# Expert layer of a decoder trunk: transpositions and gather in halves, second matrix loaded with four consecutive rows per partition

## The reference, cut to what matters

```python
def swiglu(h, w1, w3, w2):
    return (jax.nn.silu(h @ w1) * (h @ w3)) @ w2
...
def moe_swiglu(h, router, w1, w3, w2):
    logits = (h @ router).astype(F32)
    top_v, top_i = lax.top_k(logits, TOP_K)
    gates = jax.nn.softmax(top_v, axis=-1)
    ...
    for e in range(N_EXPERTS):
        y = y + swiglu(h, w1[e], w3[e], w2[e]).astype(F32) * dense_gate[..., e:e + 1]
```

## Time and profile before

| | us |
|---|---|
| median of three runs | 1545.33 |
| the profiled execution | 1544.98 |
| its span, first to last instruction | 1543.2 |
| experts, from the first piece's products to the end (608.8 to 1543.2) | 934.4 |
| second full job (724.87 to 850.48) | 125.6 |
| one small job (1073.70 to 1185.40) | 111.7 |

### The profile page before, as it was taken

One profiled execution on the slowest core, in us unless ns is written; L12 is line 12 of the kernel. 1 busy time (PEld: TensorE's weight loads), 2 busy tenths in 40 slices (PEclk: granted clock), 3 DMA queues, 4 the chain that ended last, 5 costly groups with the idle time before them and its releaser, 6 DMA issues.

```text
span 1543.2 us, 19252 instructions
## 1 busy us (share of the span) xinstructions
PE 1453.4 (94%) x7350; PEld 1154.3 (75%) x7350; DVE 1115.5 (72%) x1172; ACT 926.3 (60%) x938; POOL 51.9 (3%) x64
## 2 busy tenths in 40 slices
PE   7999999999999999999999999899899899898996
PEld 5776779999886577888888767667668677677675
DVE  1515255555362337988898899998998998998997
ACT  2222344344232134776776787897887887878885
POOL 0330000000032000000000000000000000000000
PEclk9999999999999998999999999999999999999998
DMA  9522615550833081998999999999999999999990
GB/s 323 184 87 86 223 46 180 188 186 22 269 138 110 0 339 58 350 368 325 354 368 361 348 406 402 388 388 400 392 397 383 401 396 388 404 395 385 396 374 27
DMA packets 141701, 433.46 MB, mean 281 GB/s; under 512 B 5694, under 2 KB 30420, under 8 KB 141652
## 3 DMA queue, kind: packets, MB, share of 16 engines
q1 hardware_dynamic: 141460, 432.25, 74.4%
q0 software_dynamic: 192, 0.53, 0.1%
HBM read 431.71 MB, written 1.05 MB: 280 GB/s over the span
## 4 chain that ended last, share of the span: by engine, by line
PE 60%; DVE 20%; issue 13%; ACT 5%; DMA 0%; SPq 0%; DVEq 0%; ACTq 0%
PE bank L1798 19%; DVE ring_lo L1309 14%; PE bank L1387 12%; PE bank L1364 7%; PE bank L1369 6%; PE bank L1823 4%; PE bank L1649 4%; ACT w_hi L821 3%; PE bank L1353 1%; DVE h L1154 1%; PE bank L1343 1%; PE bank L1691 1%; DVE at_hi L1281 1%; PE bank L1544 1%; ACT memT L777 1%
## 5 line engine op out<-in xcount | busy, mean ns | idle before, releaser
L1309 DVE TENSOR_TENSOR ring_lo<-ring,w_hi 128x2048 fp32r<-128x2048 f32 (+1 forms) x352 | 754.7, 2187 | 77.4 <-ACT w_hi L821 76.7
L821 ACT ACTIVATE w_hi<-ring 128x2048 fp32r<-128x2048 f32 (+1 forms) x352 | 636.4, 1842 | 171.6 <-PE bank L1798 170.7
L1798 PE MATMUL bank<-w_hi,xg 128*128 128x512 f32 x1120 | 408.2, 395 | 3.1 <-DVE ring_lo L1309 3.1
L1798 PE MATMUL bank<-ring_lo,xg 128*128 128x512 f32 x896 | 363.6, 406 | 31.4 <-DVE ring_lo L1309 27.1
L1798 PEld LDWEIGHTS bank<-w_hi,xg 128*128 128x128 f32 x1120 | 211.3, 189 | 47.3 <-DVE ring_lo L1309 3.5
L1798 PEld LDWEIGHTS bank<-ring_lo,xg 128*128 128x128 f32 x896 | 168.5, 188 | 104.4 <-DVE ring_lo L1309 71.0
L1798 PE MATMUL bank<-ring_lo,at_hi 128*128 128x512 f32 x448 | 182.1, 406 | 25.7 <-DVE at_hi L1281 24.4
L1798 PE MATMUL bank<-w_hi,at_hi 128*128 128x512 f32 x448 | 176.2, 393 | 0.0
L1798 PEld LDWEIGHTS bank<-ring_lo,at_hi 128*128 128x128 f32 x448 | 84.0, 187 | 63.9 <-DVE ring_lo L1309 47.4
L1095 DVE TENSOR_TENSOR wf_lo<-ring,wf_hi 128x1024 fp32r<-128x1024 f32 x66 | 80.5, 1223 | 60.0 <-ACT wf_hi L718 60.0
L718 ACT ACTIVATE wf_hi<-ring 128x1024 fp32r<-128x1024 f32 x66 | 69.6, 1058 | 70.4 <-PE bank L1387 68.8
(11 more groups left out here) (326 smaller groups left out, 1591.6 us busy)
## 6 DMA issues: line engine op xcount, KB each, us to landing
ring<-in_moe_w SPq DMA_DIRECT2D x168, 2048.0 KB, 9.7
ring<-in_ffn_w SPq DMA_DIRECT2D x18, 1536.0 KB, 6.8
ring<-in_w_in SPq DMA_DIRECT2D x6, 2048.0 KB, 15.1
ring<-in_w_out SPq DMA_DIRECT2D x8, 1024.0 KB, 5.0
ring<-in_ffn_w SPq DMA_DIRECT2D x3, 2048.0 KB, 7.7
ring<-in_w_in SPq DMA_DIRECT2D x4, 1024.0 KB, 15.4
ring<-in_xa_wkv SPq DMA_DIRECT2D x2, 2048.0 KB, 15.4
ring<-in_w_in SPq DMA_DIRECT2D x2, 1184.0 KB, 7.4
```

Source lines behind the costliest of these rows:

```text
L821: act.activation(w_hi[:, i % NB, 0:cols.stop - cols.start], ring[:, slot_of(u), cols], ACT.Copy)\
L1309: dve.tensor_tensor(ring_lo[slot_of(u)][:, cols], ring[:, slot_of(u), cols], w_hi[:, i % NB, 0:cols.stop - cols.start], sub).then_inc(S["l ...
L1798: ins = mm(dst[:, :], st_, mv, start=opens, stop=closes, skip_group_check=small)
```

## The change

Six edits.

1. `turn`, `small_silu`, `turned_hi`, `small_hidden` and `turned_lo` take a half x, and their semaphores count halves (`hn`) instead of chunks. In small jobs ACT's and DVE's steps for the second half stand one piece after those of the first; `rows1` of chunks 2 and 3 moves by one piece.
2. On TensorE, in small jobs, `turn(d-1, 1)` is done after the first piece of the w3 rows instead of directly behind `turn(d-1, 0)`; for chunk 3, half 0 comes after p37 as before and half 1 after p38. TensorE waits for `j_t` of each half ahead of that half's products.
3. The gather is cut: kt 0 to 3 before p40, kt 4 to 7 between p41 and p42; `j_gps` is raised after the second half.
4. The copy `hotT` moves from DVE (ahead of `gather_lo`) to ACT (ahead of `gather_hi`).
5. w2 units: partition p gets rows 4p to 4p+3, one run of 16 KB; transposition f takes columns f, f+4, f+8 ... of its half (a stationary operand read with a step of 16 bytes).
6. `keep_busy`: (6, 6) becomes (6, 3) ahead of `sel_ready`, and (4, 6) becomes (4, 4) ahead of the jobs.

```diff
-def rows1_at(d):
+def rows1_at(d, small):
-    return last_piece(1, d) + NB + 1
+    return last_piece(1, d) + NB + 1 + (small and d > 0 and CHUNKS[d - 1] == 2)
...
-def turned_at(d):
+def turned_at(d, x, small):
+    if small:
+        return JOB_PIECES - 2 + x if d == NCH - 1 else last_piece(1, d + 1) + NB + 1 + x
     return JOB_PIECES - 2 if d == NCH - 1 else last_piece(1, d + 1) + NB + 1
...
-                    sp.dma_start(dst, src.rearrange("e (k p) c -> p (e k) c", p=P)).then_inc(arrived[slot_of(u)], 16)
+                    rows_by = "e (p k) c -> p (e k) c" if w == 2 else "e (k p) c -> p (e k) c"
+                    sp.dma_start(dst, src.rearrange(rows_by, p=P)).then_inc(arrived[slot_of(u)], 16)
... (ACT; DVE has the same turns(i) with turned_lo and small_hidden)
+                def turns(i):
+                    for d in range(NCH):
+                        for x in halves(d):
+                            if i == turned_at(d, x, small) + (small or d == NCH - 1):
+                                turned_hi(d, x)
+                        for x in halves(d):
+                            if small and i == turned_at(d, x, small):
+                                small_silu(d, x)
...
+                turns(JOB_PIECES)
+                act.wait_ge(S["j_gtps"], j1)
+                act.activation(hotT[:, :, :], v3(ps[0], 0, 256, 2), ACT.Copy).then_inc(S["j_gt"], 1)
                 gather_hi(j2)
... (DVE)
-                dve.wait_ge(S["j_gtps"], j1)
-                dve.tensor_copy(hotT[:, :, :], v3(ps[0], 0, 256, 2)).then_inc(S["j_gt"], 1)
+                turns(JOB_PIECES)
                 gather_lo(j2)
... (TensorE)
-            keep_busy(6, 6)
+            keep_busy(6, 3)
...
-            def gather(n):
+            def gather(n, b):
                 pe.wait_ge(S["j_g"], n)
-                for kt in range(KT):
+                for kt in range(4 * b, 4 * b + 4):
...
-                i.then_inc(S["j_gps"], 1)
+                if b:
+                    i.then_inc(S["j_gps"], 1)
...
-            keep_busy(4, 6)
+            keep_busy(4, 4)
...
+                        if then is not None and cols.start == 0:
+                            then()
...
-                            rows = slice(FC * x + P * f, FC * x + P * f + P)
+                        rows = slice(FC * x + f, FC * x + FC, 4)
...
-                    turn(d - 1)
-                    rows_of(3, d)
-                    pe.wait_ge(S["j_t"], cn[d - 1])
+                    turn(d - 1, 0)
+                    later = None
+                    if CHUNKS[d - 1] == 2:
+                        if small:
+                            later = lambda: turn(d - 1, 1)
+                        else:
+                            turn(d - 1, 1)
+                    rows_of(3, d, later)
...
-                        products(2, d - 1, part)
-                        if d == NCH - 1 and part == 0:
-                            turn(d)
+                        later = None
+                        if d == NCH - 1 and part:
+                            turn(d, 0)
+                            if small:
+                                later = lambda: turn(d, 1)
+                            else:
+                                turn(d, 1)
+                        pe.wait_ge(S["j_t"], hn[d - 1][part])
+                        products(2, d - 1, part, later)
...
-                gather(j2)
-                pe.wait_ge(S["j_t"], cn[NCH - 1])
-                products(2, NCH - 1, 0)
-                products(2, NCH - 1, 1).then_inc(S["j_yps"], 1)
+                for part in range(2):
+                    gather(j2, part)
+                    pe.wait_ge(S["j_t"], hn[NCH - 1][part])
+                    ins = products(2, NCH - 1, part)
+                ins.then_inc(S["j_yps"], 1)
```

More of the change, by code:

```diff
@@ L38 @@
 CHUNK0 = tuple(FC * sum(CHUNKS[:d]) for d in range(NCH))
+HALF0 = tuple(sum(CHUNKS[:d]) for d in range(NCH))
+HALVES = sum(CHUNKS)
 MAX_JOBS = N_EXP + 3
@@ L768, in job @@
                 cn = [act.snap(j * NCH + (c + 1)) for c in range(NCH)]
+                hn = [[act.snap(j * HALVES + (HALF0[d] + x + 1)) for x in range(CHUNKS[d])] for d in range(NCH)]
                 j1, j2, pieces = act.snap(j + 1), act.snap(j + 2), act.snap(j * JOB_PIECES + len(FFN_PIECES))
@@ L784, in small_rows3, with small_silu, turned_hi @@
                     i.then_inc(S["j_a"], 1)
[L786 to L800, removed]
-                    i.then_inc(S["j_th"], 1)
+                def small_silu(d, x):
+                    act.wait_ge(S["j_tps"], hn[d][x])
+                    act.activation(s_sil[x], ps[4 + x][:, 0:256], ACT.Silu).then_inc(S["j_hid"], 1)
+                def turned_hi(d, x):
+                    act.wait_ge(S["j_m" if small else "j_tps"], hn[d][x])
+                    if d == NCH - 1 and x:
+                        act.wait_ge(S["j_gtps"], j1)
+                    if small:
+                        i = act.activation(at_hi[:, 4 * x:4 * x + 4, 0:SMALL], s_act[x], ACT.Copy)
+                    else:
+                        i = act.activation(at_hi[:, 4 * x:4 * x + 4, :], v3(ps[4 + x], 0, 512, 4), ACT.Copy)
+                    i.then_inc(S["j_th"], 1)
+                def turns(i):
[6 more added lines that the diff above has]
+                                small_silu(d, x)
                 for i in range(JOB_PIECES):
@@ L806, in job @@
                             yrow_out(j, half)
+                    turns(i)
                     for d in range(NCH):
[L808 to L813, removed]
+                        if i == rows1_at(d, small):
                             rows1(d)
@@ L1257, in job @@
                 cn = [dve.snap(j * NCH + (c + 1)) for c in range(NCH)]
+                hn = [[dve.snap(j * HALVES + (HALF0[d] + x + 1)) for x in range(CHUNKS[d])] for d in range(NCH)]
                 j1, j2, pieces = dve.snap(j + 1), dve.snap(j + 2), dve.snap(j * JOB_PIECES + len(FFN_PIECES))
@@ L1266, in rows3, with small_hidden, turned_lo, turns @@
                     i.then_inc(S["j_a"], 1)
[L1267 to L1271, removed]
                     for x in halves(d):
[L1273 to L1283, removed]
-                    i.then_inc(S["j_t"], 1)
+                        dve.sem_inc(S["j_m"], 1)
+                        dve.sem_inc(S["j_hid"], 1)
+                def small_hidden(d, x):
+                    dve.wait_ge(S["j_hid"], hn[d][x])
+                    dve.tensor_tensor(s_act[x], v3(s_sil[x], 0, 256, 4), v3(ps[4 + x], 256, 512, 4), mult)\
+                       .then_inc(S["j_m"], 1)
+                def turned_lo(d, x):
+                    dve.wait_ge(S["j_th"], hn[d][x])
+                    fs = slice(4 * x, 4 * x + 4)
+                    if small:
+                        i = dve.tensor_tensor(at_hi[:, fs, SMALL:P], s_act[x], at_hi[:, fs, 0:SMALL], sub)
+                    else:
+                        i = dve.tensor_tensor(at_lo[:, fs, :], v3(ps[4 + x], 0, 512, 4), at_hi[:, fs, :], sub)
+                    i.then_inc(S["j_t"], 1)
+                def turns(i):
+                    for d in range(NCH):
+                        for x in halves(d):
+                            if i == turned_at(d, x, small) + (small or d == NCH - 1):
+                                turned_lo(d, x)
+                        for x in halves(d):
+                            if small and i == turned_at(d, x, small):
+                                small_hidden(d, x)
                 for i in range(JOB_PIECES):
@@ L1771, in job, with products @@
                 cn = [pe.snap(j * NCH + (c + 1)) for c in range(NCH)]
+                hn = [[pe.snap(j * HALVES + (HALF0[d] + x + 1)) for x in range(CHUNKS[d])] for d in range(NCH)]
                 j1, j2, pieces = pe.snap(j + 1), pe.snap(j + 2), pe.snap(j * JOB_PIECES + len(FFN_PIECES))
-                def products(w, d, part):
+                def products(w, d, part, then=None):
                     u = UNIT_OF[w, d, part]
```

30 lines of the change are left out of this document (17 added, 13 removed).

## The result

Four runs of the changed kernel took 1624.97 us in the median (1615.97 to 1626.6), four of the kernel before beside them 1545.53 (1545.2 to 1546.16). The ratio is 1.0501, interval 1.0484 to 1.0519: 5% slower, where the prediction had 0.3% faster. The profiled execution has a span of 1624.8 us against 1543.2, and its mean granted TensorE clock is 0.965.

What follows compares the result with a forecast made beforehand. Full jobs were taken as bound by TensorE, small jobs by a saturated DVE with six pauses. Small jobs -3.3, full jobs +1.2 and ahead of the jobs -1.9 sum to -4.0: from 1545.33 to 1541.3 us, range 1532 to 1550.

Steps and rivals of the forecast that it cites:

- Columns f, f+4, ...: Weight loads of the turns, read with a 16-byte step: no change taken; bounds no change and half pace, doubling the turn.
- The third rival: Stepped loads in the turns at half pace: 10.5 us a small job, 63 in all; about 1610 us; 8 in 100.
- Turns in halves: Small jobs: -0.4 us each at turn(1) and turn(2); at turn(3) a 1.42 pause goes and 0.32 comes at p42.
- Gather in halves: Small jobs: pauses 2.33 at p43, 1.86 at `gather_lo`, 0.25 at p2; +0.64 with turn(3), net +0.3 with `hotT`.
- `hotT` off DVE: Small jobs: moving this copy from DVE to ACT was to save DVE 0.33 us by starts.
- Full jobs: TensorE waits 0.6 us at p40 after the gather's first half; two jobs +1.2 us, between 0 and +2.6.
- Ahead of the jobs: Three fewer idle matmuls before the selection: -1.9 us; with the clock back later, between -2.0 and +1.6.
- Runs of 16 KB: DMA of w2 units: 0 taken; faster landings worth 0, slower ones covered up to 4 us a job.
- Rival 2: Gather's second half costs more if turns give under 0.3 us a job: 1548.7 or 1550.6 us; 15 in 100.
- Rival 1: DVE's pauses at the turns vanish: 3.3 us more a small job, about 20 in all, 1521 us; 16 in 100.

## Why the prediction was wrong

**The step that failed** is "Columns f, f+4, ...": "I take no change, since the float32 load already takes some two cycles of 2.4 GHz for each column and a second line a column may fit into that." It doesn't. The upper bound given there, a load at half the pace which doubles the turn, is what came: half a turn 3.53 us for 1.75, a pair of load and matmul 0.22 us for 0.11, a load in itself 330 ns for 192. The term that was put at 0 was 85 us in the changed kernel. The argument for the lower bound rested on no row, since the trace had no load with a step; it was a guess on how two costs overlap. The prediction quotes the cacheline rule of the Trainium skill (Advanced Engine Details and Errata, "SBUF Cachelines"), by which each access on a different line pays. It spoke against the edit. The price as a mechanism of this kernel was reckoned at 65 us against a forecast gain of 4, and it was given 8 in 100. With both bounds open and nothing in the trace between them, it should have had several times that.

**The third rival** was the mechanism, and its sizes can be checked. It spoke of three turns and a half but added 3.5 x 3 = 10.5 us a small job. The doubled turns measured 12.5 us on TensorE, of which 10.75 reached the job. That 10.5 came so near is luck: one half too few was counted, and nothing was taken off for what DVE's stock still covers. It forecast 6 us for the transposes of the full jobs at 0.11 each. There the loads do get slower, as the load group of those transposes shows in the kernel after (shortest, median, longest in ns; 138, 140, 143 with contiguous columns):

```profile
L1845 PEld LDWEIGHTS bank<-cst,j_act x56: 196/211/212, 633.4 to 841.6; 128*128 128x128 f32 x56
```

but eight of them take 0.87 us instead of 0.79, so it is 0.01 each. And it left out the clock, some 11 us in the kernel with the columns alone. With 1610 - 6 + 11 it would have been 1615; measured 1625. The 10 left aren't explained by a run. The four runs of the changed kernel say that the clock has a part in them: the one with a mean clock of 0.977 took 1615.97 us, the three at 0.965 to 0.968 took 1623.58 to 1626.6.

**The rest, by the kernels with contiguous columns.** Together these steps were to give -4.0 and gave -5.4 (1540.16 against 1545.59; by the spans -4.2).
- *Turns in halves.* Pauses at turn(2) of 0.65 and 0.39, forecast 0.85 and 0.48 + 0.18; before 1.35 and 0.37. So -0.7 a turn, not -0.4. At turn(3) 0.18, forecast 0.32. The direction and the places were right, and the run with the turns joined bears out the reason.
- *Gather in halves.* p43 2.28, forecast 2.33; `gather_lo` 1.78, forecast 1.86; the next job's p2 0.13, forecast 0.25. That this edit loses was in the working (+0.64 with turn(3)), and the kernel with the gather in one block shows it. The upper bound of +2.2 there adds 0.33 for a `hotT` that gains nothing; by its own terms it is +1.9.
- *`hotT` off DVE* was to give 0.33 a small job and gave almost nothing: DVE's busy time is 104.14 against 104.15, since each of its 45 pieces takes 2194 ns instead of 2188, and its small steps also some ns more, as many as there were. Why, no run tells. DVE's pauses fell from 7.4 to 4.6 + 1.8, by 1.0, and the period by 0.90.
- *Full jobs:* the wait of p40 for `at_lo` is 0.46, forecast 0.6, but the two periods grew by 1.3 and 0.7, 2.0 for 1.2. With the gather in one block both growths are gone.
- *Ahead of the jobs:* here the later clock decided, which the prediction had only in its bounds (-2.0 to +1.6). In the profiled executions of the seven kernels with the short keep_busy it came back between 594 and 601. Where it came back at 594 (every second column), the wait for the ranks is gone as forecast (0.15 us), but DVE's own chain ran 1.0 us later in that execution, so the gather starts only 0.8 earlier (596.84 for 597.64). In the others the wait is 1.1 and the gather takes 3.9 to 5.2. The first piece comes between 607.3 and 608.9 in the seven, and between 608.2 and 609.4 in the five with the long form: 1.0 us earlier in the mean, not 1.9.
- *Runs of 16 KB:* 0, as forecast.

**Rival 2** (the second half of the gather costs more than the turns give) had a true mechanism but not the sign: the turns give -1.4 a small job, not 0.3. **Rival 1** (no pauses left at the turns) was a third true: of the 3.3 us a small job that it had beyond the forecast, 1.1 came, since 1.04 us of pause stay at each turn and 0.18 at turn(3). These are the same with the gather in one block, so the 1534.52 there is no sign for it.

## What to carry to other kernels

A step in an access pattern is a change of its own, however free the instruction count looks: if no row of the trace has the access, its two bounds are the forecast until a run of one line decides. Here a step of 8 bytes kept runs of 8 KB for 3.7 us, and a step of 16 bytes kept runs of 16 KB for 85, and neither bought anything. When work of one engine stops the supply of another, splitting it only helps if a unit of supply goes between the parts (2.2 us a job for the turns); and it costs where the next engine then waits for the last part, as DVE did for the gather in halves (1.78 us). Ask also of each edit whether anything waits for what it speeds up: here nothing waited for the landings that the larger runs made faster.

## What the hardware showed unexpectedly

- Float32 weight loads of 128 columns in the turns: 192 ns contiguous, 196 at a step of 8 bytes, 330 at 16 and 334 at 32. Those of a transpose: 140 contiguous, 209 at 8 and 211 at 16; eight transposes take 0.79 us contiguous and 0.87 at both steps. So the two uses have their jump at different steps. Why, and why the transposes hide what the turns don't, no run here tells.
- With a step of 16 bytes, load and matmul go on at 0.23 us a pair while the granted clock is 0.50, as at 1.00 (columns alone, 1032.6 to 1038.2). The pace of these loads isn't set by that clock.
- TensorE was busy 5.00 of 5 us around a turn with slow loads and was granted 0.75 there. Turns of nearly that length made of twice as many fast matmuls kept 1.00. What of the slow loads makes the grant fall stays open.
- After the same cut in filling matmuls, in front of the same work, the clock came back anywhere between 594 and 601 us in the profiled executions of seven kernels (without the cut: between 594 and 596, in five). How much of such a cut is kept varies with it.
